# Projections on x times its modulated weight, the norm's factor applied at the PSUM exit, and later first loads on GpSimd

## The reference, cut to what matters

```python
def _rmsnorm(x, g):
    y = xf * lax.rsqrt(jnp.mean(xf * xf, axis=-1, keepdims=True) + EPS)
    return (y * g).astype(x.dtype)

def _layer(x, mods, params, attend):
    sh1, sc1, gt1, sh2, sc2, gt2 = mods            # silu(c) @ w_ada + b_ada, in six parts
    h = _rmsnorm(x, g1) * (1 + sc1) + sh1
    a_in, a_b, a_c, p_in, q, k, v = jnp.split(h @ w_in_l, IN_SPLITS, axis=-1)
    y = jnp.concatenate([_short_conv(...), _multi_pool(...), attend(q, k, v)], axis=-1)
    x = x + gt1 * (y @ w_out_l)
    h = _rmsnorm(x, g2) * (1 + sc2) + sh2
    x = x + gt2 * _peer(h, wq_l, sk_l, u_l, v_l)   # queries h @ wq_l, top-k keys, all experts' gates
    return x, ctx_kv
```

## Time and profile before

| | |
|---|---|
| median of 3 executions | 2993.91 us (2993.81 to 2997.59) |
| the profiled execution | 2996.14 us, its span 2994.4 us |
| mean granted TensorE clock | 0.981 of full speed |
| TensorE busy in matmuls | 2869.4 us, 96% of the span |
| VectorE, ScalarE, GpSimd busy | 64%, 41%, 1% |
| DMA | 582.60 MB, mean 195 GB/s |

### The profile page before, as it was taken

One profiled execution on the slowest core, in us unless ns is written; L12 is line 12 of the kernel. 1 busy time (PEld: TensorE's weight loads), 2 busy tenths in 40 slices (PEclk: granted clock), 3 DMA queues, 4 the chain that ended last, 5 costly groups with the idle time before them and its releaser, 6 DMA issues.

```text
span 2994.4 us, 44821 instructions
## 1 busy us (share of the span) xinstructions
PE 2869.4 (96%) x16110; PEld 2632.3 (88%) x16110; DVE 1919.3 (64%) x4189; ACT 1216.8 (41%) x2025; POOL 25.4 (1%) x51
## 2 busy tenths in 40 slices
PE   6998999999999999999979889999999999999997
PEld 5977999999999788888878789999999998888886
DVE  3444487777875688888554445778778755555555
ACT  3343434344343444444344433443444444444443
POOL 0000000000000000000000000000000000000000
PEclk8999999999999999999989899999999999999999
DMA  6452354763856977777532124448557497666661
GB/s 278 144 216 86 127 169 131 215 196 117 274 155 228 349 280 293 290 281 294 172 113 78 57 85 153 155 122 269 153 176 243 126 304 277 213 235 219 231 224 57
DMA packets 256872, 582.60 MB, mean 195 GB/s; under 512 B 13040, under 2 KB 209904, under 8 KB 211632
## 3 DMA queue, kind: packets, MB, share of 16 engines
q1 hardware_dynamic: 251904, 546.64, 54.7%
q0 software_dynamic: 4784, 33.56, 2.8%
HBM read 476.86 MB, written 103.28 MB: 194 GB/s over the span
## 4 chain that ended last, share of the span: by engine, by line
PE 92%; DVE 3%; DMA 3%; ACT 1%; issue 1%; SPq 1%; ACTq 0%; DVEq 0%
PE ps L727 34%; PE ps L766 34%; PE ps L619 13%; PE ps L748 6%; DMA wring<-in_w_ada_dram 1%; PE ps L692 1%; DMA act_scratch<-act_h 1%; PE ps L709 1%; PE ps L681 1%; PE ps L561 1%; PE ps L662 1%; PE ps L583 1%; DMA act<-act_scratch 0%; PE ps L661 0%; DMA gate_scratch<-g_all 0%
## 5 line engine op out<-in xcount | busy, mean ns | idle before, releaser
L727 PE MATMUL ps<-h_lo,u_hi 128*128 128x384 f32 x2048 | 695.4, 340 | 14.6 <-DVE u_lo L1224 7.0
L727 PE MATMUL ps<-h_hi,u_lo 128*128 128x384 f32 x2048 | 686.9, 335 | 0.0
L727 PE MATMUL ps<-h_hi,u_hi 128*128 128x384 f32 x2048 | 685.9, 335 | 0.0
L766 PE MATMUL ps<-v_lo,w_hi 128*128 128x512 f32 x1536 | 597.8, 389 | 4.3 <-DVE v_lo L1365 3.0
L766 PE MATMUL ps<-v_hi,w_lo 128*128 128x512 f32 x1536 | 597.6, 389 | 0.0
L766 PE MATMUL ps<-v_hi,w_hi 128*128 128x512 f32 x1536 | 597.5, 389 | 0.0
L1365 DVE TENSOR_TENSOR v_lo<-wring,v_hi 128x512 fp32r<-128x512 f32 x512 | 353.8, 691 | 324.4 <-ACT v_hi L992 324.4
L992 ACT CAST v_hi<-wring 128x512 fp32r<-128x512 f32 x512 | 317.3, 621 | 549.0 <-PE ps L766 548.9
L1224 DVE TENSOR_TENSOR u_lo<-wring,u_hi 128x1024 fp32r<-128x1024 f32 x256 | 312.8, 1222 | 206.3 <-ACT u_hi L949 203.9
L727 PEld LDWEIGHTS ps<-h_lo,u_hi 128*128 128x128 f32 x2048 | 386.0, 188 | 19.2 <-DVE u_lo L1224 11.0
L727 PEld LDWEIGHTS ps<-h_hi,u_hi 128*128 128x128 f32 x2048 | 385.9, 188 | 0.0
(11 more groups left out here) (170 smaller groups left out, 2961.0 us busy)
## 6 DMA issues: line engine op xcount, KB each, us to landing
wring<-in_u_t_dram SPq DMA_DIRECT2D x128, 1024.0 KB, 5.7
wring<-in_v_t_dram SPq DMA_DIRECT2D x128, 1024.0 KB, 4.9
act_scratch<-act_h SPq DMA_DIRECT2D x256, 192.0 KB, 5.9
gate_scratch<-g_all SPq DMA_DIRECT2D x48, 1024.0 KB, 6.1
gate<-gate_scratch SPq DMA_DIRECT2D x64, 768.0 KB, 6.2
act<-act_scratch SPq DMA_DIRECT2D x64, 768.0 KB, 7.8
wring<-in_w_ada_dram SPq DMA_DIRECT2D x24, 1024.0 KB, 7.4
mod_w<-in_w_mod_dram POOLq DMA_DIRECT2D x24, 1024.0 KB, 6.9
```

The costliest lines, as they stand in the source:

```text
L727: last = nc.tensor.matmul(ps[:, 6 + s % 2, 0:T], u[:, s % 2, k], hx[:, k], start=(k == 0 and n == 0), stop=(k == KC - 1 and n == 2))
L766: last = nc.tensor.matmul(ps[:, bank + tb], w[:, group * G + b, cols], v[:, n % 4], start=(first and n in (0, G) and k == 0), stop=(last_u ...
```

## The change

It does five things.

1. `h_hi` and `h_lo` no longer hold the split of the normalised h for the first projection. They hold the split of x * g(1+sc) (`scaled_high`, `scaled_low`), which needs no norm factor, and two more columns, T and T+1, with the split of the shift of each group of tokens (`shift_high`, `shift_low`). The matmuls of the two projections take 386 columns instead of 384. For the queries the same stands in new tiles `g_hi` and `g_lo`.
2. At the PSUM exit VectorE multiplies the 386 columns by the norm's factor (1 for the last two, or the factor times the attention's scale for the q blocks) into `col_t` (`projected`, `queried`), and ScalarE adds the projected shift as a bias while it copies to the destination, in two instructions. Column blocks go to four PSUM banks in turn.
3. ScalarE casts the weights two blocks ahead before it empties a block, not after it.
4. In layer 1 the turned sums, the residual, the scaling, the first column block and the sums of squares are interleaved by k, and the first two weight blocks are split before the experts' stage ends. For the queries the scaling follows each block of the output projection, and the first query block starts before the sums are complete. The normalised second h for the experts is made between the query blocks, at blocks 6, 8, 10 and 12 (`NORM_AT`).
5. GpSimd's memsets stay at the start, but its five loads of layer 0 wait until the 8 tiles of the first modulation part were used. A wait for `branch_rdy` on TensorE moves behind three scores, `vecs` is dropped in favour of `vec_all`, and the last norm is as before.

```diff
+TS = T + 2
+TW = T + 16
+NORM_AT = (6, 8, 10, 12)
...
-    h_hi = at("h_hi", [P, KC, T], F32R)
-    h_lo = at("h_lo", [P, KC, T], F32R)
+    h_hi = at("h_hi", [P, KC, TW], F32R)
+    h_lo = at("h_lo", [P, KC, TW], F32R)
...
+            nc.gpsimd.memset(pool_in[:], 0.0).then_inc(pad_rdy.sem, 1)
+            nc.gpsimd.memset(norm_t[:, 2, T:TS], 1.0).then_inc(pad_rdy.sem, 1)
+            if l == 0:
+                pool.wait_ge(w_used.sem, w_used.at(0, N_ADA1))
+                pool.sem_inc(pool_passed.sem, 1)
             pool.dma_start(rcnt[:].rearrange("p b t -> p (b t)"), consts[:, C_RCNT:]).then_inc(mix_ld.sem, 16)
-            nc.gpsimd.memset(pool_in[:], 0.0).then_inc(pad_rdy.sem, 1)
...
+            def scaled_columns(M, bank, k, which, hi, lo, mm):
+                if k == 0:
+                    columns_split(M)
+                pe.wait_ge(gl_rdy.sem, gl_rdy.at(l, which * (KC + 1) + k + 2))
+                for n, (w, gx) in enumerate(((u_hi, lo), (u_hi, hi), (u_lo, hi))):
+                    last = nc.tensor.matmul(ps[:, bank, 0:TS], w[:, M % 2, k], gx[:, k, 0:TS], ...)
...
+            def queries(m):
+                pe.wait_ge(pq_mul.sem, pq_mul.at(l, m - 3))
+                for k in range(KC):
+                    scaled_columns(SP_WQ0 + m, pq_bank(m), k, 1, g_hi, g_lo, pq_mm)
+                    if m == 0 and k >= KC - 2:
+                        sums(2 * l + 1, (k,))
...
+                for k in range(KC + 2):            # TensorE, layer 1, first block
+                    if k < KC:
+                        added_turned(l - 1, k)
+                    if k >= 2:
+                        scaled_columns(0, pj_bank(0), k - 2, 0, h_hi, h_lo, pj_mm)
+                        sums(2 * l, (k - 2,))
...
+        def scaled_high(l, which, hi, k):
+            for v in range(2):
+                last = nc.scalar.activation(hi[:, k, seg_cols(v)], x[:, k, seg_cols(v)], ACT.Copy,
+                                            scale=gs[l][:, which, k, v:v + 1])
+            last.then_inc(gh_rdy.sem, 1)
...
             for m in range(HP):                    # ScalarE, queries
                 act.wait_ge(pq_mm.sem, pq_mm.at(l, m + 1))
-                nc.scalar.copy(pq[:, m], ps[:, m % 2, 0:T]).then_inc(pq_evac.sem, 1)
                 if m < HP - 2:
                     columns_high(l, SP_WQ0 + 2 + m)
+                if m == 0:
+                    root(2 * l + 1)
+                    act.wait_ge(kv_st.sem, kv_st.at(l, 32))
+                act.wait_ge(pq_mul.sem, pq_mul.at(l, m + 1))
+                for v in range(2):
+                    last = nc.scalar.activation(pq[:, m, seg_cols(v)], col_t[:, m % 2, seg_cols(v)], ACT.Identity,
+                                                scale=1.0, bias=col_t[:, m % 2, T + v:T + v + 1])
+                last.then_inc(pq_evac.sem, 1)
+                if m in NORM_AT:
+                    norm(l, NORM_AT.index(m))
...
+            columns_low(l, SP_WQ0 + 2)             # VectorE, queries
+            inverse_root(2 * l + 1)
+            queried(0)
+            for m in range(1, HP):
+                if m < HP - 2:
+                    columns_low(l, SP_WQ0 + 2 + m)
+                queried(m)                         # waits for block m, multiplies 386 columns into col_t
+                if m in NORM_AT:
+                    pair = NORM_AT.index(m)
+                    normalised(l, pair)
+                    gains(l, pair)
+                if m - 1 in NORM_AT:
+                    low(1, h, NORM_AT.index(m - 1))
```

More of the change, by code:

```diff
@@ L607, in columns_split @@
                     pe.sem_inc(w_used.sem, 1)
[L609 to L613, removed]
+            def scaled_columns(M, bank, k, which, hi, lo, mm):
[3 more added lines that the diff above has]
+                for n, (w, gx) in enumerate(((u_hi, lo), (u_hi, hi), (u_lo, hi))):
+                    last = nc.tensor.matmul(ps[:, bank, 0:TS], w[:, M % 2, k], gx[:, k, 0:TS],
+                                            start=(k == 0 and n == 0), stop=(k == KC - 1 and n == 2))
+                if k == KC - 1:
+                    last.then_inc(mm.sem, 1)
@@ L696, in _ @@
             pe.wait_ge(o_evac.sem, o_evac.at(l, NU))
[L697 to L700, removed]
+            output_columns()
+            for m in range(HP):
+                queries(m)
             sk = [tile_in(W_SK0[l] + i).rearrange("p k n -> p (k n)") for i in range(2)]
@@ L1064, in norm, with normalised @@
[L1064 to L1075 removed]
+        def normalised(l, pair):
+            k = 2 * pair
+            V.tensor_tensor(h[:, k:k + 2], x[:, k:k + 2], norm_t[:, 2, 0:T].unsqueeze(1).to_broadcast([P, 2, T]), ALU.mult) \
+                .then_inc(xn_rdy.sem, 1)
@@ new lines, in gains @@
+        def gains(l, pair):
+            k = 2 * pair + 1
+            dve.wait_ge(xn_rdy.sem, xn_rdy.at(l, pair + 1))
+            if l == DEPTH:
+                last = V.tensor_scalar(h[:, k], h[:, k], vec_all[:, 0, ROW_FG + k:ROW_FG + k + 1], None, ALU.mult)
+            else:
+                for v in range(2):
+                    last = V.tensor_scalar(h[:, k, seg_cols(v)], h[:, k, seg_cols(v)], gs[l][:, 1, k, v:v + 1],
+                                           mods[l][:, SH2 + k, v:v + 1], ALU.mult, ALU.add)
+            last.then_inc(hv_rdy.sem, 1)
@@ L1115, in ahead, with projected @@
-            def ahead():
-                if l == 0:
-                    modulation(0, (6,), SC1, ROW_G1)
-                columns_low(0)
-                columns_low(1)
-            norm(2 * l, 0, before=ahead)
-            for pair in range(4):
-                low(0, h, pair)
-            for M in range(2, 10):
-                columns_low(M)
+            def projected(m):
+                if m < 18:
+                    columns_low(l, m + 2)
+                dve.wait_ge(pj_mm.sem, pj_mm.at(l, m + 1))
+                dve.wait_ge(pj_evac.sem, pj_evac.at(l, m - 1))
+                V.tensor_tensor(col_t[:, m % 2, 0:TS], ps[:, pj_bank(m), 0:TS], norm_t[:, 3 if 8 <= m < 12 else 2, 0:TS], ALU.mult) \
+                    .then_inc(pj_mul.sem, 1)
```

376 lines of the change are left out of this document (228 added, 148 removed).

## The result

The changed kernel takes 2978.36 us (median of 4, 2975.85 to 2985.83) where the kernel before takes 2995.63 on the same chip: a ratio of 0.9938, with a 95% interval of 0.9921 to 0.9955. A second comparison on another chip gave 0.9939 [0.9925, 0.9954]; one execution of the kernel before took 4860 us there, at a granted clock of 0.555, and is not in that ratio. The changed kernel is faster by some 18 us. The forecast was a gain of 38.6 us, with 2970 us as the upper end of the range, so about half of the gain is missing.

The account below looks back on a forecast made before the run. TensorE, busy 96% of the span, was taken as the bound. Query stages 17.0, step to layer 1 13.5, start 6.4 and 2.5, less 0.8 for width, gave 38.6 us off 2993.9: 2955, range 2946 to 2970.

Parts of the forecast that it names:

- the last sentence of the sum: Last norm and both halves of the experts, behind the summed terms: claimed to keep their time, so no gain or loss.
- The waits: Before the fourth block of three projections: TensorE waits about 3 us, as the norm's chain now delays the exit.
- rival B: Cold stalls: the three stalls of 3.1 to 3.5 us drop the clock, 1.8 us each, giving 2960; chance 0.15.
- The width: Projection matmuls of 386 columns for 384: 0.8 ns each, times 1728 = 1.4 us, 0.6 of it counted elsewhere.
- Rival D: Projection matmuls: two odd columns cost more than two columns, at 0.5 us for each 3800 in all; chance 0.04.
- The query stage: Query projection of both layers, from the last output block to the scores: saves 8.5 us a layer, 17 in all.
- the waits while the experts' h is made between the blocks: Query blocks 6, 8, 10 and 12: ScalarE's loop lengthens by about 1.8 us each time, TensorE waits about 2.0.
- The exit loop: Exit of a column block: takes 3.7 us where TensorE needs 4.18, so it is hidden with 0.5 us to spare.
- The step to layer 1: From layer 0's experts through layer 1's first projection: first block 17.7 us earlier, then the stall; saves 13.5 us.
- The start: Kernel start to the first column block: tiles done at 32.5 against 38.9, 6.4 us saved, and 2.5 behind them.
- the moved loads: GpSimd's loads at the start: 3.15 MB, 7.5 us of DMA time ahead of the eight modulation tiles.

Follow-up runs that it names:

- the mend of the rows: Changed kernel, but experts and output projection read h through views with rows 384 elements apart, plus a 320-byte pad ahead of `h_hi`: ratio 0.9885 to the kernel before.
- both mends: Changed kernel with 384-element rows for experts and output projection, and block 3's weights split ahead of the first exit: 2960.21 us against 2998.81 before, ratio 0.9868.

## Why the prediction was wrong, point by point

**The step that failed** is the last sentence of the sum: "The last norm and both halves of the experts keep their time." I priced the tiles' new shape by its two extra columns, in the matmuls that read them. I gave no price to the readers that still take 384 columns from tiles with another row distance. Those are the experts and the output projection, 272 blocks of the kernel's 344. The runs showed that they do not keep their time: the experts' first halves lost 12.2 us in one execution and 10.5 in the other, the output projection 0.9, and the mend of the rows gave 16 back by the ratios. The term had no bounds either: the range took zero from both sides.

**The clock behind the waits.** The waits were forecast (9.5 us of them, the first at +17.4 for +17.6), the half clock behind them was rival B at 0.15. It came after all three, in every profiled execution that has the waits, at 1.5 us each where the rival had 1.8: 4.5 us. My reason against it was the earlier trace rows, 2.9 us idle at 340.3 with a full clock behind it. That was one case, not a rule (below). The rule of the Trainium skill that I had weighed, in TensorE: Matmul & The Clock Gate, section on what is actually happening, held here: the row gives 0.63 behind the wait.

**The width.** 0.8 ns a matmul was forecast from the row of 512 columns, some 4 to 5 ns are measured, 0.09 us a block or 6.5 us in 72 blocks instead of 1.4. Rival D named the right place, two columns that make an odd width, at a hundredth of its price.

**The query stage** saved 14.4 of 17.0. The half clock took 3.0 and the width of 32 blocks 2.3 beyond its price; the waits while the experts' h is made between the blocks were forecast at 2.0 a layer and came to 0.4, which gave 3.2 back. The exit loop is hidden, as forecast; its pair on ScalarE took 0.80 for my 0.98. The scores follow the last query block after 1.6 us of wait, where 1.7 were forecast.

**The step to layer 1** saved 9.2 of 13.5: 1.5 is the half clock, about 2 the width of 20 blocks. The first two blocks of weights are split early, and 1516.33 is the second block's start, 2 us later than forecast.

**The start** saved 6.2 of 8.9. That the moved loads give the tiles their time was right. The tiles were done at 34.4, not at 32.5. x came at 9.4, not at 8.3, and the DMA stood emptier than the "about a us" that I allowed:

```profile
15.00:20.00 5.00, 5.00 (x81) 3.37 (x84) 1.18 (x2) 0.52 (x1) 0.00 (x0) 1.00 0.68 285
```

With a share of 0.68, 1.6 us of DMA time are lost in this stretch. TensorE is in the sums until 18.0 and can free no slot of the ring before that; then it waits 3.3 us for the fifth tile. The rest of the 1.9 is not attributed. The first block ends 12.8 after the tiles, not 11.9.

**The account.** By the ratio 20 us are missing. The rows cost 11 to 16, the half clock 4.5, the width 5 beyond its price and the start 2.7; the shorter waits in the query stages gave 3.2 back. That makes 20 to 25. The intervals of the ratios are some 5 us wide to each side, so the account closes within them, and no closer.

## What to carry to other kernels

A tile that is made wider for one reader changes every other reader. Give the others a view with their own rows, and keep moving rows and weights alike within 256 bytes: here that was a row distance that is a multiple of 256 and tiles whose starts differ by such multiples. When a stall of some 3 us is left in a stream of matmuls, charge the half clock behind it too; work moved ahead of the late step removed both. A time per column that is read off between 384 and 512 columns said nothing of 386.

## What the runs showed of the hardware that was not expected

- A matmul's time depends on where its operands stand to each other in SBUF. A block of 24 with 384 columns takes 4.17 us when moving rows and weights stand alike within 256 bytes, 4.25 when the weights are 64 bytes off, 4.21 when rows 1600 bytes apart go through four offsets. These are blocks that stand alone; in unbroken runs with the weights 64 bytes off the cost was 0 to 0.08 us a block. Moving both by 192 bytes changes nothing. Each row is contiguous in all of these, and the granted clock is full.
- A matmul of 386 columns takes 177 to 178 ns where one of 384 takes 173 and one of 512 takes 227, at row distances of 1544, 1600 and 2048 bytes alike.
- About 3 us of idle TensorE are sometimes followed by half clock and sometimes not. At the experts' start of layer 0 the version with both mends and the changed kernel wait for the same things, TensorE being busy for 0.49 of the 3.37 us and 0.07 of the 2.94 us before it, and the clock differed, half in the first and full in the second:

```profile
330.37:334.30 3.93, 3.93 (x14) 3.93 (x15) 3.93 (x17) 1.04 (x1) 0.00 (x0) 0.61 0.59 194
```
```profile
333.94:338.00 4.06, 4.06 (x23) 4.06 (x24) 4.06 (x17) 1.05 (x1) 0.00 (x0) 1.00 0.64 210
```

  A chain of 24 expert blocks that begins so takes 102.1 us in place of 100.6. The kernel before has two (102.24 us at 541.57 and 102.22 at 2213.98). What decides was not found.
